# The opening of a two-block kernel: order of the x, c and first-weight loads, and the summing of the ada_w chunks

## The reference

```python
mod = silu(c) @ ada_w + ada_b              # c: 1 x 1024, ada_w: 1024 x 3072
shift, scale, gate = split(mod, 3)
h = rms_norm(x, norm_pre_w) * (1 + scale) + shift
z = h @ w_in                               # 1024 x 1024 by 1024 x 6144
u_pool, g_pool, q, f_pre, i_in, g_h = split(z, ...)
```

## Time and profile before

| | |
|---|---|
| median of 3 runs | 2140.09 us (2136.65 to 2140.88) |
| the profiled execution's own time | 2137.28 us |
| its span | 2135.5 us |
| TensorE, VectorE, ScalarE, GpSimd busy | 94%, 62%, 40%, 45% |
| HBM read, written | 151.71 MB, 41.16 MB |

### The profile page before, as it was taken

One profiled execution on the slowest core, in us unless ns is written; L12 is line 12 of the kernel. 1 busy time (PEld: TensorE's weight loads), 2 busy tenths in 40 slices (PEclk: granted clock), 3 DMA queues, 4 the chain that ended last, 5 costly groups with the idle time before them and its releaser, 6 DMA issues.

```text
span 2135.5 us, 27350 instructions
## 1 busy us (share of the span) xinstructions
PE 2014.2 (94%) x9969; PEld 1669.0 (78%) x9969; DVE 1331.6 (62%) x1743; ACT 848.8 (40%) x1356; POOL 952.2 (45%) x566
## 2 busy tenths in 40 slices
PE   5979999999999999989999899885999999999997
PEld 5868888888887778867888689663888888878885
DVE  6787776666637654865331543788656656556977
ACT  5434444345420034551202766456332333324453
POOL 1344553323233477733543200776655555535552
PEclk7989999999999999999999999997999999999999
DMA  9332222111122153232111000122323333247344
GB/s 276 104 109 76 65 100 85 39 29 30 50 60 60 60 172 104 99 138 61 41 47 60 20 2 9 62 99 69 103 86 106 103 118 103 83 156 258 101 135 153
DMA packets 178859, 193.95 MB, mean 91 GB/s; under 512 B 9735, under 2 KB 122840, under 8 KB 178778
## 3 DMA queue, kind: packets, MB, share of 16 engines
q1 hardware_dynamic: 172650, 178.63, 26.3%
q10 hardware_dynamic: 6128, 14.26, 1.8%
HBM read 151.71 MB, written 41.16 MB: 90 GB/s over the span
## 4 chain that ended last, share of the span: by engine, by line
PE 78%; DVE 11%; ACT 4%; issue 3%; POOL 2%; SPq 1%; DMA 1%; ACTq 0%; DVEq 0%; POOLq 0%
PE psum L957 7%; PE psum L1489 6%; PE psum L1490 6%; PE psum L1491 6%; PE psum L959 6%; PE psum L958 6%; PE psum L1120 3%; PE psum L1400 3%; PE psum L1557 3%; PE psum L1559 3%; PE psum L1558 3%; PE psum L978 3%; PE psum L977 3%; PE psum L979 3%; PE psum L1389 2%
## 5 line engine op out<-in xcount | busy, mean ns | idle before, releaser
L758 POOL TENSOR_TENSOR w_hi<-w_raw,ones 128x1024 fp32r<-128x1024 f32 x60 | 147.1, 2452 | 504.5 <-PE psum L959 375.9
L957 PE MATMUL psum<-h_hi,w_hi 128*128 128x512 f32 x704 | 284.2, 404 | 0.0
L959 PE MATMUL psum<-h_hi,w_lo 128*128 128x512 f32 x704 | 274.8, 390 | 0.0
L958 PE MATMUL psum<-h_lo,w_hi 128*128 128x512 f32 x704 | 274.2, 390 | 0.0
L1589 ACT ACTIVATE arena<-psum 128x1024 f32<-128x1024 f32 (+7 forms) x135 | 100.7, 750 | 221.0 <-PE psum L959 135.3
L761 POOL TENSOR_TENSOR w_lo<-w_raw,w_hi 128x1024 fp32r<-128x1024 f32 x60 | 161.9, 2698 | 4.7
L958 PEld LDWEIGHTS psum<-h_lo,w_hi 128*128 128x128 f32 x704 | 132.5, 188 | 28.4 <-issue 2.6
L957 PEld LDWEIGHTS psum<-h_hi,w_hi 128*128 128x128 f32 x704 | 132.4, 188 | 28.4 <-issue 2.6
L959 PEld LDWEIGHTS psum<-h_hi,w_lo 128*128 128x128 f32 x704 | 132.1, 188 | 28.5
L1557 PE MATMUL psum<-w_hi,h_hi 128*128 128x512 f32 x308 | 121.5, 394 | 8.0 <-DVE h_lo L2996 5.1
L1558 PE MATMUL psum<-w_lo,h_hi 128*128 128x512 f32 x308 | 121.1, 393 | 0.0
(11 more groups left out here) (410 smaller groups left out, 5307.9 us busy)
## 6 DMA issues: line engine op xcount, KB each, us to landing
w_raw<-w_in SPq DMA_DIRECT2D x66, 512.0 KB, 3.9
act_op<-arena SPq DMA_DIRECT2D x77, 256.0 KB, 2.1
arena<-act_op SPq DMA_DIRECT2D x77, 256.0 KB, 2.7
w_raw<-w_gate SPq DMA_DIRECT2D x22, 512.0 KB, 4.0
w_raw<-w_up SPq DMA_DIRECT2D x22, 512.0 KB, 5.2
arena<-ada_w SPq DMA_DIRECT2D x16, 512.0 KB, 7.4
arena<-w_out SPq DMA_DIRECT2D x16, 512.0 KB, 6.1
out_T<-arena SPq DMA_DIRECT2D x16, 512.0 KB, 5.8
```

Source lines behind the costliest of these rows:

```text
L957: pe.matmul(o, wh, xh, start=(k == 0), stop=False)
L958: pe.matmul(o, wh, xl, start=False, stop=False)
L959: return pe.matmul(o, wl, xh, start=False, stop=(k == KT - 1))
```

## The change

SyncE now issues x tiles 4, 6, 0 and 2, then c and the small vectors, chunks 0 to 2, the second halves (k = 4 to 7) of the four first weight tiles, each after a wait for that tile's first half, chunk 3, and the others as buffers come free. ScalarE issues its four x tiles, then the identity and the first halves (k = 0 to 3) of the four tiles. The second halves count on `lnrow_in`, for which ScalarE and GpSimd wait before k = 4. Chunk 0 is summed by TensorE alone, 16 one-column products with `silu_c`. Chunks 1 to 7 are summed by VectorE in two chains, even and odd slices, that are added at the end. VectorE and TensorE are one chunk ahead of the products in place of two. KEEP_WARM goes from 24 to 44.

```diff
--- before.py
+++ after.py
@@ -190,7 +190,8 @@
 T_END = 8 * KT
 
 X_BANKS = 7
-KEEP_WARM = 24
+KEEP_WARM = 44
+ACC_OPS = KT + 1
 CHUNK_BUFS = 4
 GATE_PARTS = 2 * KT + 2
 
@@ -301,10 +302,11 @@
         RC = 20
 
         chunk_w = lambda c: page(ADA + 2 * (c % CHUNK_BUFS), 2).rearrange("p (k c) -> p k c", c=2 * P)
-        chunk_acc = lambda c: page(ACC)[:, 2 * P * (c % 4):2 * P * (c % 4 + 1)]
+        chunk_acc = lambda c, e: page(ACC)[:, 2 * P * (2 * (c % 2) + e):2 * P * (2 * (c % 2) + e + 1)]
         first_ = rounded_pages("first_", FIRST_W, 4).rearrange("p (u e c) -> p u e c", e=2, c=PAGE)
         first_hi, first_lo = [first_[:, :, e, :] for e in range(2)]
         first_raw = page(FIRST_RAW, 2).rearrange("p (u c) -> p u c", c=PAGE)
+        first_raw_k = lambda s: (first_raw if s < 2 else w_raw)[:, s, :].rearrange("p (k c) -> p k c", c=P)
         gate_part = [page(GATE_W)[:, h * HALF:(h + 1) * HALF] for h in range(2)]
         acc_mm = psum[:, X_BANKS, P:P + 2 * KT]
         gate_row = page(GATE_ROW)
@@ -521,11 +523,9 @@
                 sp.dma_start(dst, src).then_inc(raw_in[s], 16)
 
 
+            for t in (4, 6, 0, 2):
+                load_x0(t)
             sp.dma_start(c_col, ap["c"].rearrange("a (k p) -> p (a k)", p=P), allow_slow_non_contiguous=True).then_inc(c_in, 16)
-            load_x0(4)
-            load_x0(6)
-            load_chunk(0)
-            sp.dma_start(ident[:], ap["k_ident"]).then_inc(const_in, 16)
             for name, n in VEC:
                 r = VROW[name]
                 src = ap[name]
@@ -535,13 +535,17 @@
                 else:
                     flat = src.rearrange("a (r c) -> (a r) c", c=P)
                 sp.dma_start(arena[r:r + n, VECS * PAGE:VECS * PAGE + P], flat).then_inc(vec_in, 16)
-            load_x0(0)
-            load_x0(2)
+            for c in range(3):
+                load_chunk(c)
             for s, c in enumerate((C_F, C_GH, C_V, C_Q)):
-                load(s, first_raw[:, s, :].rearrange("p (k c) -> p k c", c=P) if s < 2 else slot_fm(s), w_in_fm[c])
-            for c in range(1, KT):
-                if c >= CHUNK_BUFS:
-                    sp.wait_ge(ada_acc, KT * (c - CHUNK_BUFS + 1))
+                sp.wait_ge(raw_in[s], 16)
+                sp.dma_start(first_raw_k(s)[:, KT // 2:, :], w_in_fm[c][:, KT // 2:, :]).then_inc(lnrow_in, 16)
+            load_chunk(3)
+            for c in range(CHUNK_BUFS, KT):
+                if c == CHUNK_BUFS:
+                    sp.wait_ge(mod_mm, 2)
+                else:
+                    sp.wait_ge(ada_acc, ACC_OPS * (c - CHUNK_BUFS))
                 load_chunk(c)
             for s in range(2):
                 sp.wait_ge(first_ready, 1)
@@ -565,7 +569,7 @@
                 sp.wait_ge(tw_sent, 64 * h + 64)
 
             load_head(1, range(2, 4))
-            sp.wait_ge(ada_acc, KT * KT)
+            sp.wait_ge(ada_acc, ACC_OPS * (KT - 1))
             sp.wait_ge(tr_full, 2 * KT)
             load_t(0)
             with sp.Fori(2, T_GROUPS + 1) as h:
@@ -765,6 +769,8 @@
                 pool.wait_ge(raw_in[s], 16)
             for k in range(KT):
                 at = slice(k * P, (k + 1) * P)
+                if k == KT // 2:
+                    pool.wait_ge(lnrow_in, 64)
                 pool.wait_ge(w_rounded, 2 * k + 1)
                 x = TT(w_lo[:, :, at], first_raw[:, :, at], w_hi[:, :, at].bitcast(F32), ALU.subtract)
                 x.then_inc(first_ready, 1) if k < KT - 1 else x.then_inc(w_ready, 2)
@@ -1036,10 +1042,20 @@
 
             def chunk_sums(c):
 
-                pe.wait_ge(ada_acc, KT * (c + 1))
-                pe.wait_ge(mod_done, 2 * c if c else 1)
+                pe.wait_ge(ada_acc, ACC_OPS * c)
+                pe.wait_ge(mod_done, 2 * c)
                 for a in range(2):
-                    mm = pe.matmul(acc_mm[:, 2 * c + a:2 * c + a + 1], chunk_acc(c)[:, a * P:(a + 1) * P], ones[:, 0:1], start=True, stop=True)
+                    mm = pe.matmul(acc_mm[:, 2 * c + a:2 * c + a + 1], chunk_acc(c, 0)[:, a * P:(a + 1) * P], ones[:, 0:1], start=True, stop=True)
+                mm.then_inc(mod_mm, 1)
+
+            def first_chunk_sums():
+
+                pe.wait_ge(ada_in[0], 32)
+                pe.wait_ge(silu_done, 1)
+                pe.wait_ge(mod_done, 1)
+                for a in range(2):
+                    for k in range(KT):
+                        mm = pe.matmul(acc_mm[:, a:a + 1], chunk_w(0)[:, k, a * P:(a + 1) * P], silu_c[:, k:k + 1], start=(k == 0), stop=(k == KT - 1))
                 mm.then_inc(mod_mm, 1)
 
             def first_weights(u):
@@ -1062,11 +1078,9 @@
             x_transposes(1)
             pe.wait_ge(vec_in, 16 * len(VEC))
             pe.transpose(psum[:, X_BANKS, 0:VROWS], arena[0:VROWS, VECS * PAGE:VECS * PAGE + P], ident[0:VROWS, 0:VROWS]).then_inc(mod_mm, 1)
-            pe.wait_ge(ones_set, 1)
-            chunk_sums(0)
+            first_chunk_sums()
             pe.wait_ge(xn_done, NT)
             x_transposes(0)
-            chunk_sums(1)
 
 
             V, KD, ATTN, SST = page(B_V), page(B_KD), page(B_ATT), page(B_S)
@@ -1175,8 +1189,8 @@
             for i in range(2 * KT - X_BANKS, 2 * KT):
                 pe.wait_ge(*xt_taken(i))
             for k in range(KT):
-                if k + 2 < KT:
-                    chunk_sums(k + 2)
+                if k + 1 < KT:
+                    chunk_sums(k + 1)
                 if k < KT - 1:
                     pe.wait_ge(first_ready, 2 * k + 2)
                 else:
@@ -1591,6 +1605,9 @@
 
             for t in (5, 7, 1, 3):
                 act.dma_start(tiles(X0)[:, t, :], ap["x"][0, t * P:(t + 1) * P, :]).then_inc(x_in[t], 16)
+            act.dma_start(ident[:], ap["k_ident"]).then_inc(const_in, 16)
+            for s, c in enumerate((C_F, C_GH, C_V, C_Q)):
+                act.dma_start(first_raw_k(s)[:, 0:KT // 2, :], w_in_fm[c][:, 0:KT // 2, :]).then_inc(raw_in[s], 16)
             act.wait_ge(c_in, 16)
             A(silu_c, c_col, ACT.Silu).then_inc(silu_done, 1)
 
@@ -1663,6 +1680,8 @@
                 if k >= 2:
                     act.wait_ge(lo_done, 2 * k - 2)
                 A(page(WHOLE[k % 2]), spare_lo[:, k, :], ACT.Identity, scale=mul_a[:, k:k + 1], bias=mod[:, k:k + 1]).then_inc(hi_done, 1)
+                if k + 2 == KT // 2:
+                    act.wait_ge(lnrow_in, 64)
                 if k + 2 < KT:
                     first_round(k + 2)
             act.wait_ge(lb_step, 1)
@@ -2250,12 +2269,19 @@
                 dve.tensor_copy(spare_lo[:, k, half * HALF:(half + 1) * HALF], psum[:, i % X_BANKS, :]).then_inc(xt_dve, 1)
 
             def chunk_sum(c):
+
+                base = ACC_OPS * (c - 1)
                 dve.wait_ge(ada_in[c % 4], 32 * (c // 4 + 1))
-                w, acc = chunk_w(c), chunk_acc(c)
-                TS(acc, w[:, 0, :], silu_c[:, 0:1], None, ALU.mult).then_inc(ada_acc, 1)
-                for k in range(1, KT):
-                    dve.wait_ge(ada_acc, KT * c + k)
-                    STT(acc, w[:, k, :], silu_c[:, k:k + 1], acc, ALU.mult, ALU.add).then_inc(ada_acc, 1)
+                w = chunk_w(c)
+                for k in range(KT):
+                    acc = chunk_acc(c, k % 2)
+                    if k < 2:
+                        TS(acc, w[:, k, :], silu_c[:, k:k + 1], None, ALU.mult).then_inc(ada_acc, 1)
+                    else:
+                        dve.wait_ge(ada_acc, base + k - 1)
+                        STT(acc, w[:, k, :], silu_c[:, k:k + 1], acc, ALU.mult, ALU.add).then_inc(ada_acc, 1)
+                dve.wait_ge(ada_acc, base + KT)
+                TT(chunk_acc(c, 0), chunk_acc(c, 0), chunk_acc(c, 1), ALU.add).then_inc(ada_acc, 1)
 
             def chunk_shift(c):
                 dve.wait_ge(mod_mm, c + 2)
@@ -2272,8 +2298,6 @@
             x_rstd(1)
             for t in (4, 5, 6, 7):
                 x_scale(t)
-            dve.wait_ge(silu_done, 1)
-            chunk_sum(0)
             x_stats(0)
             for k in (0, 2):
                 xt_copy(1, k)
@@ -2284,14 +2308,15 @@
             for k in (4, 6):
                 xt_copy(1, k)
             chunk_shift(0)
-            chunk_sum(1)
             for k in (1, 3, 5, 7):
                 xt_copy(0, k)
-            for k in range(KT):
-                if k + 2 < KT:
-                    chunk_sum(k + 2)
+            dve.wait_ge(silu_done, 1)
+            chunk_sum(1)
+            low_part(0)
+            for k in range(1, KT):
+                chunk_shift(k)
                 if k + 1 < KT:
-                    chunk_shift(k + 1)
+                    chunk_sum(k + 1)
                 low_part(k)
             lower_bounds()
 
@@ -2744,7 +2769,7 @@
                 TS(mean, sums, -1.0 / ATT, None, ALU.mult).then_inc(mean_done, 1)
                 dve.wait_ge(var_done, NT)
                 stats(M_LN, ss[:, 0:8], ATT, LN_EPS)
-                dve.wait_ge(lnrow_in, 32)
+                dve.wait_ge(lnrow_in, 96)
                 for t in range(NT):
```

## The result

The changed kernel takes 2145.09 us (median of 12 runs, 2143.43 to 2148.97), the kernel before 2136.78 us on the same chip (12 runs, 2134.49 to 2140.88). The ratio is 1.0041 [1.0034, 1.0049]: **slower by 8.3 us** between the medians (7.3 to 10.5 by the interval of the ratio). The forecast was +3.0 and 2143.1, in a range of 2134 to 2149.5: sign and range hold, the size is too small. That 2143.1 comes within 2 us of 2145.09 is in part luck: it starts from a median of 2140.09 over three runs, and over twelve the kernel before stands at 2136.78, from where +3.0 gives 2139.8.

A forecast was written before the change was run, and what follows sets the result against it. TensorE, busy 94% of the span, was taken as the bound, fed by a chain of waits in the first 95 us. +2.1 at T0 and +1.1 after made +3.2, taken as +3.0: 2143.1 us, range 2134 to 2149.5.

The forecast's parts named there:

- c behind x: Opening loads: c lands at 16.5 us behind four x tiles, so first transposes come at 26.3, 8.5 us later.
- Rival 4: Opening loads: c is not held up by x and lands by 8 us; -5.2 us, 2134.9; chance 0.20.
- ScalarE's own issues: Opening: ScalarE's five new load issues end before c lands, costing nothing; with c early they would hold squares 3.4 us.
- 32 records: TensorE's 16 one-column products for chunk 0, between the two rounds of transposes; 4.0 us at the high clock.
- the forecast of the clock: TensorE's clock, after the second transposes' former pattern, is up at 31 us, by the time of chunk 0's products.
- the second transposes: TensorE's second round of 32 transposes, after chunk 0's products; 3.3 us at the high clock, copies done at 41.0.
- the first sum: VectorE's two-chain sum of chunk 1 after the copies; 4.23 us, including 0.7 for GpSimd working beside it.
- T0: Start of the first product of the first weights on TensorE; 44.30 us before, claimed 46.4, +2.1 us.
- the stage: First 95 us: x becomes h and the first four weight tiles run, ending at head 1's first product, 94.29 before.
- From T0 on: First-weight products until the last one: 51.05 us in place of 49.99, +1.1 us, with a period of 5.65.
- Rival 3: VectorE's sums: two chains give no overlap, 0.55 us more per sum; +3.6 us, 2146.7; chance 0.12.
- VectorE's lead: At T0 VectorE is one chunk ahead instead of two, so its pace is no longer covered by a lead.

The follow-up runs named there:

- Experiment 1: The changed kernel with c's load issued by SyncE before x tiles 4, 6, 0, 2 instead of behind them; 2140.54 us, ratio 1.0022.
- Experiments 3: The changed kernel with c issued first and the first halves of the four weight tiles issued by SyncE instead of ScalarE; 2137.45 us, ratio 1.0001.
- experiment 6: The kernel before with chunk 0 summed by TensorE alone in 16 one-column products, VectorE's sum 0 left out; 2140.99 us, ratio 1.0022.
- experiment 5: The kernel before with all eight chunk sums of VectorE in two chains added at the end; 2133.71 us, ratio 0.9990.
- first try of experiment 8: The kernel before with two chains, c first, then all SyncE x tiles, chunks 0 and 1 ahead of the first weights; 2132.78 us, ratio 0.9984.
- experiment 2: The kernel before with SyncE issuing x tiles 4, 6, 0, 2 and then c; 2140.95 us, ratio 1.0022.

## Why the prediction was right in sign and small in size

**c behind x: right.** Silu at 16.13 (16.5 said), first transposes 25.75 (26.3), copies done 41.35 (41.0). Rival 4 fell: c is held up with weights on the other queue and without. The trace agrees with the Trainium skill's rule that one ring's descriptors are consumed in order (DMA: Bandwidth & Descriptors, Queues, rings and completion order): c is there at 14.2 and 16.1 us behind the four x tiles of its own queue, and at 5.3 or earlier ahead of them, with the other queue's x tiles in flight each time.

**ScalarE's own issues: right for the change, where c comes later still.** The prediction gave them nothing for that reason, and said that with c early they would hold the squares up to 11.5. Experiment 1 measured 11.27 for the end of the issues, but 12.68 for the first square: the table load of 1.28 us stands behind the issues too, and the prediction left it out. So the issues are a second cost that c's lateness hid, and undoing c's place alone gives back only 3.6 us.

**32 records: right here because of the clock that they met.** They took 3.70 us (4.0 said). Experiments 3 and 6 measured 5.41 and 6.96 for the same instructions at lower clocks, so the forecast of the clock was partly luck. Beside it, the second transposes were a miss: 5.36 us where 3.3 were said, since the clock fell again at 36 (granted 0.55); that they started 1.9 us earlier than said hid it.

**The step that failed is the size of the first sum,** 4.23 us, with "0.7 where GpSimd works beside it" in it. It took 6.3. The 0.7 came from a sum in the kernel before that had two GpSimd operations beside it. In the change VectorE has a single sum ahead of T0, and it starts just when ScalarE's rounding releases six of them. The two scalings went from 0.61 to 1.64 and the six steps from 2.46 to 4.32. With 6.3 in that term the prediction's own sum gives T0 +4.2 and +5.3 for the end of the stage; the profile has +4.6 and +5.75. Of the 5.3 us that the forecast of +3.0 lacks against the median's 8.3, this term is 2.1. Of the rest, 0.5 is in the stage, 0.7 behind it in the profile, 1.9 between the profiles and the medians, and 0.2 was rounded off the sum.

**From T0 on: right in sum.** The stretch took 51.15 us (51.05 said), with a period of 5.8 (5.65) from k = 2 to 5 and 5.2 from there to k = 6, in front of which TensorE no longer waits. The parts inside a period were off in both directions: GpSimd's two operations fall on the end of the sum and on the low part, so the sum takes 3.8 us (4.23 said) and the low part 1.7 (1.15).

**Rival 3 fell.** Starts of two chains' steps are 0.41 apart, less than the 0.48 that one step takes. No semaphore is left out for that: each step waits for the one before the last instead of for the last. The Trainium skill (VectorE: DVE Perf Modes, The DRAIN you can't avoid) says that the next operation does not start until the pipe is empty, but in the same place that one that "is not held starts earlier". The prediction used only the first half and took it for rival 3's rule. The trace of experiment 5 agrees with the second half, with a sum of 3.4 us in place of 4.0.

**VectorE's lead was not priced by itself.** With two chunks ahead and all eight sums on VectorE (experiment 5) the same stretch takes 48.5 us: five sums are left after T0 in place of six, and VectorE's last low part behind a sum comes 27.3 us after T0 (70.41) instead of 34.2 (83.12). That is 2.6 us less; how much of it is the lead and how much the place of chunk 0 was not tried.

**What the medians say together,** each against the kernel before: the change +8.3; with c first +4.7; with the weights off ScalarE's queue too +1.1; with GpSimd off the sum too −1.5. What is then left of the change still holds chunk 0 on TensorE (+4.7 alone) and the two chains (−2.2 alone), so the parts do not simply add up. The first try of experiment 8, with the chains and c first but without the TensorE part, has −3.6. One term stays open. After the stage the distance between matching products of the two traces moves between 3.5 and 6.6 us and ends at 6.4; in experiment 2 it goes from 1.2 up to 4.3 and ends at 2.0. Two traces thus differ after the stage, where the kernels do the same work, by as much as some of the parts are worth, and one trace of each kernel can't place the 1.9 us by which the median exceeds the span.

## What to carry to other kernels

- Issue a tiny load that everything waits for ahead of the bulk loads of its queue (here 3.6 us of medians).
- Do not let an engine that has to compute next issue bulk loads: while an issue stands, the engine computes nothing (here another 3.6 us).
- Price an operation at its new place. Read what else runs in the stretch where it will stand (GpSimd beside VectorE, TensorE's clock), above all when only one copy of it is left on the path.
- Moving work from an engine that waits anyway to the one on the path is a loss even if the work is short (experiment 6).

## What the runs showed that was not expected

- GpSimd's work stretches VectorE's by very different amounts: two scalings from 0.61 to 1.64 us, six steps from 2.46 to 3.41 (two of GpSimd's operations beside them) or 4.32 (four beside them, two beside the scalings), the low part from 1.22 to 1.75.
- An issue can stand on its engine for long: 6.57 us for two DMAs of 256 KB on ScalarE, 5.90 us for one small vector on SyncE right behind c's 1024 pieces, and 9.83 us for the two DMAs of chunk 0 behind c in experiment 2. That it waits for room in its queue is read from what stands ahead of it and was not tried by itself.
- TensorE's granted clock was 0.55 in 36 to 38 us, under transposes that followed 10 us of nearly unbroken work, while in the first try of experiment 8 the second transposes ran at 1.00 (32 in 3.71 us). The same opening thus moves by several us with the placing, and no run here gives the rule.
- A longer warm-up made the first transposes fast (28 in 3.22 us) and the whole not faster: 2135.05, 2.3 us over the same kernel without it.
